# Head of a hybrid mixer and expert layer: eight slots for the token tiles, modulation rows in turns with the transposes, and expert passes with the high part of the weights first

## What is computed

```python
m  = silu(c) @ w_mod + b_mod                # six rows of 1024; the context uses two of them, from c_ctx
h  = rms_norm(x, norm_mix_g) * (1 + sc) + sh
h_c = rms_norm(ctx, norm_mix_g) * (1 + sc_c) + sh_c
p  = h @ w_in                               # gMLP part, q, o, k, v and the gates
x  = x + g * (concat(gmlp(p), mlstm(p, state from h_c)) @ w_out)
h2 = rms_norm(x, norm_ffn_g) * (1 + sc2) + sh2
gate, idx = top_k(softmax(h2 @ w_router), 128)     # each of 16 experts takes 128 tokens
ye = (silu(xe @ w_gate) * (xe @ w_up)) @ w_down * gate     # xe: (128, 1024), expert width 2048
out = rms_norm(x + g2 * scatter_add(ye), final_g)
```

## Time and profile before

| | us |
|---|---|
| median of three runs | 1795.7 (1795.26 to 1799.47) |
| the profiled execution | 1796.74 |
| its span in the trace | 1794.9 |
| PE, DVE, ACT busy | 1671.7, 1348.8, 1043.0 |

### The profile page before, as it was taken

The page is one execution under the profiler, slowest core; times in us unless marked ns, Lnnn a source line. Parts: engine busy times, 40 slices in busy tenths (PEclk is TensorE's granted clock), DMA queues, the critical chain, the costliest instruction groups (busy, mean ns, idle before and its releaser), DMA issues.

```text
span 1794.9 us, 21845 instructions
## 1 busy us (share of the span) xinstructions
PE 1671.7 (93%) x8224; PEld 1368.6 (76%) x8224; DVE 1348.8 (75%) x1305; ACT 1043.0 (58%) x960; POOL 146.4 (8%) x137
## 2 busy tenths in 40 slices
PE   5989999999889609999999999999999999999995
PEld 2579997888767508888888888888888888888884
DVE  2556543417854488889888898888898898899897
ACT  5253122236432307777777777777777777777775
POOL 3001100002100000101101101001011011011010
PEclk9899999999989859999999999999999999999998
DMA  9115631021222628999999999999999999999996
GB/s 340 55 33 158 194 106 48 24 70 48 85 82 100 251 83 325 359 390 383 369 398 372 372 395 371 380 390 369 381 390 368 384 387 369 388 387 366 389 378 243
DMA packets 204424, 492.81 MB, mean 275 GB/s; under 512 B 5700, under 2 KB 18792, under 8 KB 204376
## 3 DMA queue, kind: packets, MB, share of 16 engines
q1 hardware_dynamic: 188128, 436.35, 65.4%
q0 software_dynamic: 13248, 47.09, 8.7%
q10 hardware_dynamic: 3000, 8.70, 1.2%
HBM read 471.07 MB, written 21.05 MB: 274 GB/s over the span
## 4 chain that ended last, share of the span: by engine, by line
PE 87%; DVE 8%; ACT 2%; issue 1%; DMA 1%; ACTq 0%; DVEq 0%; POOL 0%; POOLq 0%
PE ps L1073 83%; PE ps L1479 2%; PE ps L1442 1%; DVE topi L1966 1%; DVE topv L1965 1%; DVE affT L1968 1%; DVE hs L1821 1%; DVE ring L2049 1%; PE ps L1091 0%; PE ps L1398 0%; ACT h2T L969 0%; DVE wl L2016 0%; ACT hs L909 0%; DVE bns L1839 0%; DVE wol L1873 0%
## 5 line engine op out<-in xcount | busy, mean ns | idle before, releaser
L2016 DVE TENSOR_TENSOR wl<-ring,wh 128x2048 fp32r<-128x2048 f32 x384 | 877.8, 2290 | 111.0 <-ACT wh L1017 110.8
L1017 ACT ACTIVATE wh<-ring 128x2048 fp32r<-128x2048 f32 x384 | 736.9, 1920 | 286.5 <-PE ps L1073 286.5
L1073 PE MATMUL ps<-wh,xel 128*128 128x512 f32 x1024 | 408.1, 398 | 1.4 <-DVE xel L1996 1.4
L1073 PE MATMUL ps<-wh,xeh 128*128 128x512 f32 x1024 | 401.6, 392 | 0.0
L1073 PE MATMUL ps<-wl,xeh 128*128 128x512 f32 x1024 | 400.9, 392 | 0.0
L1073 PEld LDWEIGHTS ps<-wh,xeh 128*128 128x128 f32 x1024 | 192.5, 188 | 45.0
L1073 PEld LDWEIGHTS ps<-wh,xel 128*128 128x128 f32 x1024 | 192.6, 188 | 42.7 <-DVE xel L1996 1.8
L1073 PEld LDWEIGHTS ps<-wl,xeh 128*128 128x128 f32 x1024 | 192.7, 188 | 41.1
L1073 PE MATMUL ps<-wh,hidl 128*128 128x512 f32 x512 | 204.0, 398 | 0.0
L1073 PE MATMUL ps<-wh,hidh 128*128 128x512 f32 x512 | 200.8, 392 | 0.0
L1073 PE MATMUL ps<-wl,hidh 128*128 128x512 f32 x512 | 200.3, 391 | 0.0
(11 more groups left out here) (367 smaller groups left out, 1997.6 us busy)
## 6 DMA issues: line engine op xcount, KB each, us to landing
ring<-in_w_gate_e SPq DMA_DIRECT2D x64, 2048.0 KB, 8.6
ring<-in_w_up_e SPq DMA_DIRECT2D x64, 2048.0 KB, 8.2
ring<-in_w_down_e SPq DMA_DIRECT2D x64, 2048.0 KB, 10.0
mbw<-in_w_mod POOLq DMA_DIRECT2D x32, 512.0 KB, 5.1
hpr<-in_w_in SPq DMA_DIRECT2D x12, 1024.0 KB, 5.4
moda<-in_w_mod SPq DMA_DIRECT2D x4, 2048.0 KB, 19.6
xs<-in_x POOLq DMA_DIRECT2D x8, 512.0 KB, 7.0
wor<-in_w_out SPq DMA_DIRECT2D x2, 2048.0 KB, 8.1
```

The lines of the kernel that those rows point to most:

```text
L1017: act.activation(whv[m % 4], eview(m), ACT.Copy).then_inc(hi_done, 1)
L1073: return pe.matmul(o, l, r, start=start, stop=stop)
L2016: dve.tensor_tensor(wlv[m % 4], eview(m), whv[m % 4].bitcast(F32), ALU.subtract).then_inc(lo_done, 1)
```

## The change

- **Slots and banks.** `xs` has eight slots of 4 KB per partition (four in the region of `hpr[1]`) and the transposes three pairs of banks.
- **Queues.** POOL issues tiles 0 and 1, then sets the constants, then issues tiles 2 to 7, the gates, and tiles 8 and 9 after the transposes of tiles 0 and 1. SP no longer waits for tiles: it loads half of piece 0 at once, ACT's queue loads the other half; SP goes on with piece 1 when both have landed. The second `hpr` piece waits for the transpose of tile 7.
- **Head order.** New lists for PE and DVE and one for ACT. Rows 0 run ahead of all tiles; rows 1 behind tile 4. The copy of a transposed tile is split: ACT takes the first bank, DVE the second.
- **Around the wave.** The context's `hch` is made ahead of the copy of `wsT`, the `wsraw` transposes go into the wave behind k = 5, and `piece_low(0)` moves behind `h_shift(1)`.
- **Experts.** A half runs its eight passes on `wh` after a wait for `hi_done` and then its four on `wl` after a wait for `lo_done`.
- Some semaphores are shared (`x_in`, `gains_in`, `xe_in`) with the counts to match.

```diff
-        HEAD_PE = "t0 t1 t2 t3 r0 t4 t5 c0 r1 t6 t7 t8 t9 c1 r2".split()
-        HEAD_DVE = "t0 t1 t2 t3 t4 t5 r0 t6 t7 c0 t8 r1 t9 c1".split()
+        HEAD_PE = "r0 t0 t1 t2 t3 t4 c0 r1 t5 t6 c1 t7 t8 t9 r2".split()
+        HEAD_ACT = "t0 t1 t2 t3 e0 e1 t4 e2 t5 e3 e4 t6 t7 g t8 t9 e5 e6 e7 e8 e9 w".split()
+        HEAD_DVE = "t0 t1 t2 t3 r0 e0 e1 t4 e2 e3 c0 t5 e4 t6 t7 g t8 t9 r1 e5 e6 c1 e7 e8 e9".split()
...
-            for t in range(4, NTC + NT):
-                pool.wait_ge(xt_ready, t - 3)
-                pool.dma_start(xs[:, t % 4, :], xf[(t - NTC) * P:(t - NTC + 1) * P, :]).then_inc(x_in[t % 4], 16)
+            for t in range(XS, NTC + NT):
+                pool.wait_ge(xt_ready, t - XS + 1)
+                pool.dma_start(xs[t % XS][:], xf[(t - NTC) * P:(t - NTC + 1) * P, :]).then_inc(x_in[t % XS], 16)
...
-            sp.wait_ge(x_in[1], 16)
-            mod_piece(0)
-            sp.wait_ge(x_in[3], 16)
+            a = MOD_ORDER[0] * W
+            sp.dma_start(moda[0][:, 0:KT // 2], wmod[:, 0:KT // 2, a:a + W]).then_inc(mod_in[0], 16)
+            sp.wait_ge(mod_in[0], 32)
             mod_piece(1)
             half_piece(0)
             mod_piece(2)
             mod_piece(3)
+            sp.wait_ge(xt_ready, XS)
             half_piece(1)
...
+            a = MOD_ORDER[0] * W
+            act.dma_start(moda[0][:, KT // 2:], wmod[:, KT // 2:, a:a + W]).then_inc(mod_in[0], 16)
...
+            act.wait_ge(h_mod, 2 * KT)
+            act.activation(hch[:], hcr[:], ACT.Copy).then_inc(h_hi, 1)
             act.wait_ge(ws_t, 1)
             act.activation(wsT[:], ps[:, 6, :].rearrange("p (h q) -> p h q", h=H), ACT.Copy).then_inc(wsT_ready, 1)
-            act.wait_ge(h_mod, 2 * KT)
-            act.activation(hch[:], hcr[:], ACT.Copy).then_inc(h_hi, 1)
...
-                if t >= 2:
-                    pe.wait_ge(xt_free, t - 1)
+                if t >= 3:
+                    pe.wait_ge(xt_free_a, t - 2)
+                    pe.wait_ge(xt_free_v, t - 2)
...
-                    pe.wait_ge(lo_done, e * (2 * EC) + m + 1)
+                    pe.wait_ge(hi_done, e * (2 * EC) + m + 1)
...
-                            last = mm3(o, xeh[:, k], xel[:, k], whv[m % 4][:, kk * W:(kk + 1) * W],
-                                       wlv[m % 4][:, kk * W:(kk + 1) * W], k == 0, k == KT - 1)
+                            w = whv[m % 4][:, kk * W:(kk + 1) * W]
+                            mm(o, xeh[:, k], w, k == 0, False)
+                            mm(o, xel[:, k], w, False, False)
+                        pe.wait_ge(lo_done, e * (2 * EC) + m + 1)
+                        for kk in range(hk):
+                            k = hf * hk + kk
+                            last = mm(o, xeh[:, k], wlv[m % 4][:, kk * W:(kk + 1) * W], False, k == KT - 1)
...
+            def token_copy(t):
+
+                dve.wait_ge(xt_ready, t + 1)
+                hk = KT // 2
+                dst = hcr[:, hk:, t * P:(t + 1) * P] if t < NTC else hTr[:, hk:, (t - NTC) * P:(t - NTC + 1) * P]
+                dve.tensor_copy(dst, ps[:, tbank(t) + 1, :].rearrange("p (k t) -> p k t", k=hk)).then_inc(xt_free_v, 1)
...
-            piece_low(0)
-            dve.wait_ge(xt_free, NTC + NT)
+            dve.wait_ge(xt_free_a, NTC + NT)
+            dve.wait_ge(xt_free_v, NTC + NT)
...
             h_shift(0)
             h_shift(1)
+            piece_low(0)
             h_low(0)
+            h_low(1)
             mod_copy(2)
-            h_low(1)
```

More of the change, by code:

```diff
@@ L291, in hybrid_block @@
         gates_in = sem("gates_in")
-        x_in = [sem(f"x_in{i}") for i in range(4)]
+        x_in = [sem(f"x_in{i}") for i in range(XS)]
         mod_in = [sem(f"mod_in{i}") for i in range(MOD_A)]
@@ L491, in num_view, with tbank @@
             return ps[:, 4 + b, 0:2 * V1].rearrange("p (a v) -> p a v", v=V1)
-        XS_TURNS = [len(range(i, NTC + NT, 4)) for i in range(4)]
+        XS_TURNS = [len(range(i, NTC + NT, XS)) for i in range(XS)]
+        def tbank(t):
+            return 2 * (t % 3)
         block = es.enter_context(nc.Block())
@@ L499, in _, with head_consts @@
             link = chain(pool, pool_step)
-            for t in range(4):
-                src = cf[t * P:(t + 1) * P, :] if t < NTC else xf[(t - NTC) * P:(t - NTC + 1) * P, :]
[L502 to L516, removed]
+            def head_consts():
+                link(pool.memset(ident[:], 0.0))
+                link(pool.affine_select(out=ident[:], in_=ident[:], compare_op=ALU.not_equal, fill=1.0, base=0,
+                                        pattern=[[-1, P]], channel_multiplier=1))
+                pool.memset(ones[:], 1.0)
+                pool.memset(epsc[:], EPS)
+                pool.tensor_copy(identb[:], ident[:])
+                pool.memset(floorc[:], LOG_INV_SCALE)
+                pool.memset(raw[:, 0:1], 0.0)
+                pool.memset(raw[:, T + 1:T + 2], 0.0)
+                pool.memset(rawc[:, 0:1], 0.0)
+                pool.memset(rawc[:, TC + 1:TC + 2], 0.0)
+                link(pool.memset(gbias[:], 0.0))
+                link(pool.memset(wgr[:], 0.0))
+                pool.sem_inc(consts_in, 1)
+            for t in range(XS):
+                src = cf[t * P:(t + 1) * P, :] if t < NTC else xf[(t - NTC) * P:(t - NTC + 1) * P, :]
+                pool.dma_start(xs[t][:], src).then_inc(x_in[t], 16)
+                if t == 1:
+                    head_consts()
             for n in range(4):
@@ L729, in piece_high @@
                 act.activation(hph[i % 2][:], hpr[i % 2][:], ACT.Copy).then_inc(hp_hi, 1)
[L731 to L743 removed]
+            for what in HEAD_ACT:
+                if what == "g":
+                    gates_high()
+                elif what == "w":
                     piece_high(0)
[L745 removed]
+                else:
+                    {"t": token_square, "e": norm_copy}[what[0]](int(what[1:]))
             for k in range(KT):
@@ L1153, in _ @@
                     mod_cols(3)
-            pe.wait_ge(ws_in, 16)
-            pe.wait_ge(moda_ready, 4)
-            for h in range(H):
-                last = pe.transpose(ps[:, 6, h * P:(h + 1) * P], wsraw[:, h], ident[:])
-            last.then_inc(ws_t, 1)
+                if k == 5:
+                    pe.wait_ge(ws_in, 16)
+                    pe.wait_ge(moda_ready, 4)
+                    for h in range(H):
+                        last = pe.transpose(ps[:, 6, h * P:(h + 1) * P], wsraw[:, h], ident[:])
+                    last.then_inc(ws_t, 1)
             pe.wait_ge(h_lo, KT + 1)
```

106 lines of the change are left out of this document (55 added, 51 removed).

## The result

| | us |
|---|---|
| median after | 1772.07 (1771.06 to 1775.87, 4 executions) |
| median before, same chip | 1797.59 (1795.26 to 1800.08, 4 executions) |
| ratio | 0.9862, 95% interval 0.9848 to 0.9876 |
| profiled execution after | 1772.78, span 1771.0 |
| the same two kernels on another chip, later | 1777.00 (4) against 1798.69 (7): 0.9884, 0.9867 to 0.9900 |

The forecast was 1779.5 with a range from 1773 to 1788. The first comparison gave a gain of 25.5 us, the second 21.7; the forecast had 16.2. The direction was right, the size was not: the first measurement lies 0.9 us under the range. The later one lies inside it, with 5.5 us more of gain than forecast.

The account below looks back on a forecast made before the run. PE's passes and their pace were taken to bound the experts, the head being judged by when the wave starts and ends. Terms -11.4 (head), -4.8 (wave's end) and 0 (experts) sum to -16.2: 1795.7 to 1779.5 us, range 1773 to 1788.

Parts of the forecast that it names:

- Rows 0: Head: PE starts rows 0 at 13.0 us, at latest 15.2, and they take 9.07 us.
- Wave start: End of the head: the wave starts at 48.0 us in place of 59.36, -11.4 us.
- End of the wave: Wave's end: PE's wait on hcl goes, -4.8 us; the wsraw transposes are the same four wherever they stand.
- Behind it ACT and DVE are no later with respect to PE than now: Middle, wave's end to first expert pass: moves as a block and stays as long as now, 566.8 us.
- rival B: Head slower than laid out: rows 1 and 2 each start at low clock, 4.1 us; range 1784 to 1788, chance 0.20.
- Experts, 0: Experts: same 288 passes per expert, the added wait and new order cost or gain 0.
- The lower bound: Experts: if the new order reached the wave's 0.2267 us per pass, 4608 passes would give -14.3 us.
- The wait in mid half: Experts: 384 added waits for the low part in the middle of each half, taken as 0.
- C: Experts: the wait in mid half holds PE up, 0.09 us each, +34.6, giving 1814 us; chance 0.06.
- D: Experts: the order of passes changes PE's pace, down to 1765 or up to 1793.8 us; chance 0.05 and 0.04.
- E: Head: DVE's chain becomes the bound, the wave starts no earlier, only 4.8 us remain, 1790.9; chance 0.08.
- A: Whole kernel: the terms as summed hold, 1775.5 to 1784 us; chance 0.57.

Follow-up runs that it names:

- the run with the wave's end alone: Kernel before with only hch ahead of wsT on ACT and the wsraw transposes behind k = 5: 1790.0 us, ratio 0.9954.
- Low passes first: Changed kernel with each half's four wl passes ahead of its eight wh passes: 1773.2 us, later 1775.8 us on another chip.
- early rows: Changed kernel with rows 0 starting on piece 0's first half, pieces 1 and 2 issued earlier, wl passes first in experts: 1773.9 us, ratio 0.9860.

## Why the prediction was right and wrong

- **Rows 0** (13.0, then 9.07): 13.62 and 9.52, so 0.6 and 0.4 later; the upper bound of 15.2 was passed in four later profiles (15.38, 15.90, 15.92, 16.30). The 385 GB/s were read as those of one POOL and one SP queue; ACT's queue had `wsraw` under way as well (3.54 to 10.60), which changes nothing in the sum. Pieces 1 and 2 landed at 28.11 and 39.98, 1 and 2 us later than laid out, and still 1.3 and 1.4 us ahead of their rows. **Tiles 0 to 3** (3.9) 3.72; **tile 4** (wait, start 27.1): waits 1.29, starts 28.07, 5.0 us behind the end of rows 0, as forecast. **Rows 1 and 2** 7.03 each, as taken. **Wave start** 48.0: 48.36. The term was 11.4 and measured 11.0.
- **End of the wave** (-4.8): -4.94. The amount was right, one reason was not: the order on ACT alone gives only 2.8 (46.34 to 43.53); the move of the transposes, written off as neutral, gives the other 2.2.
- **"Behind it ACT and DVE are no later with respect to PE than now"**, and with it the 566.8 us of the middle "as long as now": the step that failed first. The block did not move as a whole. Its beginning had been at 1.2 GHz, as a result of the stall that the change takes out, and this is worth 1.6 us, shown by the run with the wave's end alone. The window at clock 0.50 could have been read in the trace of before; the forecast took the clock into account where it might cost (rival B) and not where it could give something back. The other 1.6 us of the middle (523.48 to 521.90) are within what the same program scatters by (521.90 and 524.63 in two profiles of the changed kernel), and nothing shows them to be due to the change.
- **Experts, 0**: the mis-sized term. It measured -4.8 (0.32 us per expert over 15, and 1085.29 to 1080.45 over the stretch). The lower bound was derived from the right row, the wave's pace, -14.3 at most; a third of it came. The sentence that failed is "I see no reason for it: the operands and the writers are the same". They are, but the sequence of the passes was not, and the sequence counts. The zero left unexplained what the rows had shown: the experts' own pace of 0.2298 against the wave's 0.2267 was a difference on passes of the same size and in the same order of `mm3`. What makes that difference is still open; what the runs show is that reordering the passes moves the experts' pace by 0.5% either way (kernel before with the new order, changed kernel with the old one).
- **The wait in mid half**, 0: right, 0.00 with and without it.
- **The tail**: unchanged, 37.13 and 37.20.

In sum: 11.0 and 4.9 where 11.4 and 4.8 were forecast; 1.6 and 4.8 missed; 1.6 by chance in the profiled pair.

The rivals. **B** (rows 1 and 2 at the low clock behind tiles) fell: 7.03 both. The rule that speaks for it agrees with two runs and not with the tiles of the kernel before; in the changed kernel rows 0 had brought PE to full pace, and the tightly placed tiles behind them kept it (3.72 for four, 1.97 for two). **C** fell with the run without the wait. **D**, downward, is what happened, a third of the way; it had been given 0.05. **E** fell: DVE's list holds PE up only once, for 1.29 us. The range missed because A's own width was for the head alone, while D downward and A together, 1775 and below, were not taken in.

Low passes first (1775.8 and 1773.2) and early rows (1773.9) do not beat the changed kernel (1772.1 and 1777.0) by anything that these runs show.

## What to carry to other kernels

When a change removes a stall of PE of some microseconds, look at the granted clock in the window behind it: here a stall of 4.8 us cost 6.4. When passes are reordered, don't put the pace at "unchanged" because all operands are the same; compare the pace of two stages with passes of the same size, and if they differ, the difference is a term of the sum with a chance of its own. And when a step moves to another place in one engine's list, follow its result into the lists of the others: what is the same work for PE was the head of ACT's queue.

## What was not expected of the hardware

- In the experts the pace of passes with 512 columns hangs on the order in which they read two groups of buffers: 2.72 to 2.79 us for 12 passes, fixed for each buffer and order and reproducible to 0.01 us, whether DVE (in both orders) and ACT (in the changed one) write beside it or not. Alternating `wl` and `wh` pass by pass costs 68.91 to 68.94 us per expert, grouping them 68.49 to 68.59. Why some buffers are free of it is open, and so is why the wave alternates in the same way at 0.2267 us per pass.
- A stall of 2.0 us cost almost as much behind it as one of 4.8: 43.24 and 43.30, against 41.69 without one (one profile of each kernel).
- 16 or 22 small transposes ran at the pace of clock 0.50 (1.2 GHz) throughout and did not bring rows 0 to full pace, though in the kernel before the fast pace came behind 16 transposes of tiles. The clock column of the profile reads 1.00 there: at the start of an execution durations have to be read beside it.
- A transfer issued 7.5 us earlier, on engines that are full and with the next piece issued right behind it, landed 0.2 us earlier; the next piece, issued 8.1 us earlier, landed 4.0 us earlier.
